# A decoder layer in float32: the first MLP matrix by seven products on half the tokens

## The reference

```python
h = rms_norm(x, norm_mix_pre[l])
m = hybrid_mixer(h, ...)                 # three parallel branches, gated, one output projection
x = x + rms_norm(m, norm_mix_post[l])
h = rms_norm(x, norm_ffn_pre[l])
f = jnp.square(jax.nn.relu(h @ w_ff1[l])) @ w_ff2[l]      # 1024 -> 4096 -> 1024
x = x + rms_norm(f, norm_ffn_post[l])
```

## Time and profile before

| | |
|---|---|
| Time, median of 3 runs | 987.01 us (986.59 to 987.07) |
| Profiled execution | 986.88 us; span from first to last instruction 985.1 us |
| TensorE busy | 965.7 us, 98% of the span, 4380 matmuls |
| VectorE, ScalarE, GpSimd busy | 674.5, 382.4, 98.6 us |
| MLP, first to last matmul | 645.36 to 977.43 us |
| DRAM read / written | 120.75 / 2.10 MB |

### The profile page before, as it was taken

One profiled execution on the slowest core, in us unless ns is written; L12 is line 12 of the kernel. 1 busy time (PEld: TensorE's weight loads), 2 busy tenths in 40 slices (PEclk: granted clock), 3 DMA queues, 4 the chain that ended last, 5 costly groups with the idle time before them and its releaser, 6 DMA issues.

```text
span 985.1 us, 12346 instructions
## 1 busy us (share of the span) xinstructions
PE 965.7 (98%) x4380; PEld 803.9 (82%) x4380; DVE 674.5 (68%) x829; ACT 382.4 (39%) x493; POOL 98.6 (10%) x115
## 2 busy tenths in 40 slices
PE   5999999999999999999999999999999999999996
PEld 4888888888888888888888888898888888888885
DVE  5348888889888988886584444656665674575568
ACT  5323333333333222224274223436534534543543
POOL 3000000000000001222200000220100100010012
PEclk9999999999999999999999999999999999999998
DMA  6323332232232222224226324155576487386453
GB/s 214 123 86 108 97 106 91 85 112 90 85 108 89 86 85 85 85 86 149 86 88 233 121 92 128 65 171 159 136 220 169 97 211 226 92 201 208 120 109 104
DMA packets 34629, 123.35 MB, mean 125 GB/s; under 512 B 4000, under 2 KB 4128, under 8 KB 34592
## 3 DMA queue, kind: packets, MB, share of 16 engines
q1 hardware_dynamic: 28368, 100.84, 29.8%
q0 software_dynamic: 5120, 17.83, 10.2%
q10 hardware_dynamic: 1104, 4.19, 1.2%
HBM read 120.75 MB, written 2.10 MB: 125 GB/s over the span
## 4 chain that ended last, share of the span: by engine, by line
PE 97%; DVE 1%; DMA 1%; issue 0%; ACT 0%; POOL 0%; POOLq 0%; DVEq 0%; ACTq 0%
PE ps L1147 31%; PE ps L1151 31%; PE ps L1149 31%; PE ps L1190 1%; PE ps L1304 1%; PE ps L1305 1%; PE ps L1303 1%; DMA conf<-x_in 1%; DVE wide L1080 0%; PE ps L1253 0%; PE ps L1254 0%; DVE wide L1093 0%; PE ps L1252 0%; DVE a_lo L765 0%; ACT ps L546 0%
## 5 line engine op out<-in xcount | busy, mean ns | idle before, releaser
L765 DVE TENSOR_TENSOR w_lo<-raw,w_hi 128x1024 fp32r<-128x1024 f32 x130 | 160.4, 1237 | 114.2 <-ACT w_hi L521 113.9
L1147 PE MATMUL ps<-a_hi,w_hi 128*128 128x512 f32 x576 | 225.4, 391 | 0.0
L1149 PE MATMUL ps<-a_lo,w_hi 128*128 128x512 f32 x576 | 224.2, 389 | 0.0
L1151 PE MATMUL ps<-a_hi,w_lo 128*128 128x512 f32 x576 | 224.1, 389 | 0.0
L521 ACT ACTIVATE w_hi<-raw 128x1024 fp32r<-128x1024 f32 x130 | 137.0, 1056 | 194.1 <-PE ps L1151 125.0
L842 DVE SCALAR_TENSOR_TENSOR conf<-glu,cols,conf (+1 forms) x240 | 186.9, 779 | 27.5 <-DVE conf L842 26.4
L1147 PE MATMUL ps<-b_hi,w_hi 128*128 128x512 f32 x360 | 140.2, 390 | 0.0
L1151 PE MATMUL ps<-b_hi,w_lo 128*128 128x512 f32 x360 | 140.1, 389 | 0.0
L1149 PE MATMUL ps<-b_lo,w_hi 128*128 128x512 f32 x360 | 140.1, 389 | 0.0
L1149 PEld LDWEIGHTS ps<-a_lo,w_hi 128*128 128x128 f32 x576 | 108.2, 188 | 22.6 <-issue 0.5
L1147 PEld LDWEIGHTS ps<-a_hi,w_hi 128*128 128x128 f32 x576 | 108.2, 188 | 22.6 <-DVE w_lo L765 0.2
(11 more groups left out here) (154 smaller groups left out, 1191.2 us busy)
## 6 DMA issues: line engine op xcount, KB each, us to landing
raw<-units_in SPq DMA_DIRECT2D x134, 512.0 KB, 3.3
glu<-units_in POOLq DMA_DIRECT2D x24, 512.0 KB, 5.5
raw_v<-units_in SPq DMA_DIRECT2D x22, 512.0 KB, 4.4
raw_c<-units_in SPq DMA_DIRECT2D x20, 512.0 KB, 4.0
glu<-units_in SPq DMA_DIRECT2D x8, 512.0 KB, 5.2
glu<-rows_in ACTq DMA_DIRECT2D x4, 512.0 KB, 10.7
conf<-x_in SPq DMA_DIRECT2D x4, 512.0 KB, 7.9
conf<-x_in ACTq DMA_DIRECT2D x1, 2048.0 KB, 9.1
```

What stands on the lines that cost most here:

```text
L765: return nc.vector.tensor_tensor(dst, src, hi, ALU.subtract)
L1147: nc.tensor.matmul(ps[:, bank, :], left_hi, right_hi, start=first, stop=False, skip_group_check=on_top)
L1149: nc.tensor.matmul(ps[:, bank, :], left_hi, right_lo, start=False, stop=False, skip_group_check=on_top)
L1151: return nc.tensor.matmul(ps[:, bank, :], left_lo, right_hi, start=False, stop=final, skip_group_check=on_top)
```

## The change

The up part uses seven products as well. The 1024 input channels and the 1024 hidden channels of a quarter are halved, and the tokens into 256 and 256. An up product has two units of 24 matmuls: 2 x 4 k-blocks x 3 on 256 tokens. There are 14 up units in a quarter instead of eight, and 28 in all instead of 22.

- The token side of the seven products (three plain blocks, four sums or differences, `xs_hi` and `xs_lo`) is made once, at the hand-off and in quarter 0's up part (`x_turned`, `x_difference_hi`, `x_lo`), and kept for all quarters.
- Hidden blocks `h11`, `h12`, `h21`, `h22` are sums of products: ScalarE copies a product out of PSUM (`keep`), VectorE adds another (`join`); relu, square, differences, and the seven sets of the down part follow (`rectify`, `difference`, `minus`, `set_hi`, `set_lo`).
- Products run in the order of `ORDER`; every down product goes by token tiles, and down product 2 stays in PSUM over all quarters (`is_read`).
- Raw slots are ten: up and down have slots of their own for the blocks that get additions. The two new ones lie in `conf`, so the mixed rows are stored to DRAM (`mixed_kept`) and loaded again for the end (`back`).
- Adding transfers: 16 in a quarter instead of 8; loads 16 instead of 18.

```diff
+ORDER = ((1, 2, 5, 3, 6, 7, 4), (5, 1, 2, 3, 6, 7, 4))
+SET_OF = {1: "11", 2: "12", 4: "22", 5: "22-21", 3: "21+12-11-22", 6: "21-22-11", 7: "11-21"}
+LOADED = {1: (0, 0), 2: (1, 0), 3: (1, 1), 5: (0, 0)}
+ADDED = {5: (0, 1), 6: (1, 1), 4: (1, 0), 7: (0, 1)}
+def slot_of(f, product):
+    return {1: 0, 2: 2, 3: 6, 7: 6}.get(product, 8 if f == DOWN else 4)
...
+            ff_load(0, UP, 1)
+            ff_load(0, UP, 2)
+            ff_load(0, UP, 5)
+            for c in range(CH):
+                sp.wait_ge(mixed_in, 4 * c + 4)
+                sp.dma_start(kept_d[c * P:(c + 1) * P, :], resid[:, c, :]).then_inc(mixed_kept[c], 16)
...
             for q in range(QUARTERS):
-                add_blocks(q, (5,))
-                add_blocks(q, (6,))
-                add_blocks(q, (7,))
-                add_blocks(q, (4,))
+                add_block(q, UP, 6)
+                if q == 0:
+                    add_block(0, DOWN, 5)
+                add_block(q, UP, 7)
+                add_block(q, UP, 4)
+                if q < QUARTERS - 1:
+                    add_block(q + 1, UP, 5)
+                for product in (6, 7, 4):
+                    add_block(q, DOWN, product)
+                if q < QUARTERS - 1:
+                    add_block(q + 1, DOWN, 5)
...
+            def keep(q, product, name, h=None):
...
+                nc.scalar.activation(dst, src, ACT.Copy).then_inc(kept, 1)
+            def rectify(q, n, name, sign):
+                h = h_of[name][:, :, :]
+                nc.scalar.activation(h, h, ACT.Relu, scale=sign).then_inc(rectified, 1)
+                act.wait_ge(rectified, 4 * q + n)
+                nc.scalar.activation(h, h, ACT.Square).then_inc(hidden, 1)
...
+                for h in range(2):
+                    done(q, UP, 7, h)
+                    split_behind(q, UP, 7, h)
+                act.wait_ge(hidden_diff, 4 * q + 1)
+                set_hi(q, "22-21")
+                act.wait_ge(joined, 5 * q + 5)
+                rectify(q, 3, "11", -1.0)
+                act.wait_ge(hidden, 4 * q + 3)
+                set_hi(q, "11")
...
+            def join(q, product, name, h=None):
...
+                nc.vector.tensor_tensor(at, src, at, ALU.add).then_inc(joined, 1)
...
+                    elif product == 7:
+                        dve.wait_ge(mlp_sum, sums_after(q, product, 1))
+                        for c in (0, 1):
+                            weigh(c, 1)
+                        dve.wait_ge(out_weighted, 4)
+                        for n in range(2):
+                            finish(n)
...
+            def up_unit(q, product, h, between=None):
+                u = ff_unit(q, UP, product, h)
+                hi, low = xs_hi[SET_OF[product]], xs_lo[SET_OF[product]]
+                ready(Count(u))
+                for e in range(2):
+                    out = ps[:, up_bank(q, product) + h, e * HALF_T:(e + 1) * HALF_T]
+                    free = on(product) or e == 1
+                    for k in range(CH):
+                        w = slice((CH * e + k) * P, (CH * e + k + 1) * P)
+                        nc.tensor.matmul(out, w_hi[:, u % RING, w], hi[:, k, :], start=not free and k == 0,
+                                         stop=False, skip_group_check=free)
...
+                    if e == 0 and between:
+                        between()
...
+                elif product in (3, 6):
+                    pe.wait_ge(kept, 5 * q + {3: 3, 6: 1}[product] + h)
+                elif product in (7, 4):
+                    pe.wait_ge(joined, 5 * q + {7: 2, 4: 4}[product] + h)
```

More of the change, by code:

```diff
@@ L114 @@
[L114 to L132, removed]
@@ L135, in ff_loads @@
[L135 to L141, removed]
-def source(u, added=False):
-    q, k = divmod(u - U_FF, PER_QUARTER)
-    product, h = piece_of(u)
-    if product is None:
-        return U_FF + 2 * KT * q + k
-    k_half, n_half = (ADDED if added else LOADED)[product]
-    return U_FF + 2 * KT * q + KT + CH * n_half + 2 * k_half + h
+HALF_T = SEQ // 2
@@ new lines, in earlier_in_slot, with ff_loads, sums_in_slot, source @@
+def earlier_in_slot(u):
+    return [v for v in range(U_FF, u) if ff_slot(v) == ff_slot(u)]
+def ff_loads(u):
+    before = U_FF // RAW if ff_slot(u) < RAW else 0
+    return 16 * (before + sum(piece_of(v)[2] in LOADED for v in earlier_in_slot(u)) + 1)
+def sums_in_slot(u):
+    return 16 * (sum(piece_of(v)[2] in ADDED for v in earlier_in_slot(u)) + 1)
+def source(u, added=False):
+    q, f, product, h = piece_of(u)
+    k_half, n_half = (ADDED if added else LOADED)[product]
+    if f == DOWN:
+        k_half = 1 - k_half
+    at = 2 * (2 * k_half + n_half) if f == UP else CH * n_half + 2 * k_half
+    return U_FF + (2 * q + f) * BLOCK_UNITS + at + h
@@ L280, in build, with set_over @@
[L280 removed]
+        raw_d = over("raw_d", [P, 2, D], "conf", 2 * D)
+        slots = [raw[:, 0, :], raw[:, 1, :], raw_v[:, 0, :], raw_v[:, 1, :], weighted, row[2],
+                 row[0], row[1], raw_d[:, 0, :], raw_d[:, 1, :]]
+        def set_over(name, first, skip=0, many=4):
+            return over(name, [P, many, CH, HALF_T], first, skip * D, dt=F32R)
+        x_plain_hi, x_plain_lo = set_over("x_plain_hi", "b_hi"), set_over("x_plain_lo", "b_lo")
@@ L1073, in half_of, with difference @@
+            def difference(q, n, first, second):
+                nc.vector.tensor_tensor(h_of[first if n == 1 else second][:, :, :], h_of[first][:, :, :],
+                                        h_of[second][:, :, :], ALU.subtract).then_inc(hidden_diff, 1)
             def half_of(n_half):
@@ new lines, in _ @@
+                split_behind(q, UP, 5, 1)
+                if q == 0:
+                    x_lo("21-22-11", 10)
+                set_lo(q, "22")
+                done(q, UP, 3, 0)
+                split_behind(q, UP, 3, 0)
+                if q == 0:
+                    x_lo("11-21", 11)
+                done(q, UP, 3, 1)
+                split_behind(q, UP, 3, 1)
+                dve.wait_ge(kept, 5 * q + 5)
+                for h in range(2):
+                    done(q, UP, 6, h)
+                    join(q, 6, "21", h)
+                    split_behind(q, UP, 6, h)
@@ new lines, in _ @@
+                done(q, UP, 7, 0)
+                dve.wait_ge(kept, 5 * q + 4)
+                join(q, 7, "11", 0)
+                dve.wait_ge(hidden, 4 * q + 2)
+                dve.wait_ge(set_lo_ready, len(H_ORDER) * q + 1)
+                difference(q, 1, "22", "21")
+                split_behind(q, UP, 7, 0)
+                done(q, UP, 7, 1)
+                join(q, 7, "11", 1)
+                split_behind(q, UP, 7, 1)
+                set_lo(q, "22-21")
+                set_lo(q, "11")
```

619 lines of the change are left out of this document (383 added, 236 removed).

## The result

The changed kernel takes 990.9 us (989.7 to 991.0, 7 runs), the kernel before 987.1 us on the same chip (986.6 to 987.2, 7 runs). The ratio is 1.0035, 95% interval 1.0025 to 1.0046: slower by 0.35%. The prediction said 984.6 us. The time lies inside its range, but the change went the other way.

What follows compares the result with a forecast made beforehand. The prediction took TensorE's matmul pace to bound the MLP. From the profiled 986.88 us it summed -17.5 + 3.8 + 10.5 + 0.9 to 984.6 us, range 975 to 996.

Steps and rivals of the forecast that it cites:

- Term 1: MLP matmuls: 256-column up matmuls at 0.1200 us each shorten the MLP from 332.1 to 314.6 us, -17.5 us.
- Term 2: Turn from up to down: VectorE's late splits stall TensorE before down product 2, 1.4 + 3 x 0.8 = +3.8 us.
- Term 3: Quarter 0's up part: queued adding transfers land late, the eighth at 688.2 us, delaying product 4; +10.5 us.
- Term 4: End of the program: VectorE reaches the last addition later, behind product 7's sums, weighting and two row finishings; +0.9 us.
- No effect for later quarters' transfers: Later quarters: additions go out in turn with the slots, the tightest found landing 4 us early; no cost, term 0.
- The turn rival: Turns from up to down: 2.3 us each instead of 0.8, or TensorE's half clock adds 4.5; 990 us, chance 0.14.
- Additions in time: Quarter 0's queue: it drains faster as stores and loads overlap, costing 3 instead of 10.5; 977 us, chance 0.17.
- DMA in every quarter: Every quarter: loads and additions don't overlap, so TensorE waits for DMA in each; 995 us, chance 0.12.
- both other paces: 256-column matmuls at the load pace, 0.112 (974 us, chance 0.02), or above the line, 0.131 (999 us, chance 0.05).
- The Trainium skill's gap: 256-column matmuls: N / 2.4 + 2.5 ns, 109 ns each, a first term of about -32 us; chance 0.02.

Runs made afterwards that it cites:

- plain transfers: Changed kernel with six of quarter 0's eight up-product additions, those behind the clearing, issued as plain transfers of the same pieces: 986.3 us, ratio 0.9988.
- the half-clock run: Changed kernel with 24 extra matmuls of 256 columns, result unread, ahead of up product 7's waits in quarter 0: 989.6 us, ratio 1.0027.
- the mix: Changed kernel without ScalarE's last-quarter waits for products 7 and 4, quarter 0's down product 5 additions one behind each of up product 4's: 980.5 us.
- the turn: Changed kernel with VectorE's fourth hidden difference moved behind the two splits that down product 2 waits for: 992.9 us, ratio 1.0053.

## Why the prediction was wrong

- **Term 1, the pace (-17.5): right.** 336 matmuls of 256 columns take 40.31 us in each of quarters 1 to 3, 0.1200 each. The line through 384 and 512 columns holds down to 256; whatever holds 128 columns at 0.1117 does not show there.
- **Term 2, the turn (+3.8): right, 3.3.** 0.75, 0.74, 0.70 and 1.07 by quarter, over the 38.08 that 168 matmuls of a down part take, released by VectorE's remainder, as the step said. Quarter 0 had no 1.4; there VectorE was no later than elsewhere. The working was too heavy in one place: VectorE is busy for 25.1 us in quarter 1's up part, where the step counted 29.8.
- **Term 3, quarter 0's additions (+10.5): the size right, 11.0 (9.8 to 10.5 in other traces with the same quarter 0), by two errors that cancel, which is luck.** The last split started at 685.57, so the eighth addition had landed some 2.6 us earlier than the 688.2 of the step; the queue drained faster than the step took it, and no run splits that between loads and additions. The clock then fell to half for 27 matmuls, which the step had taken as 0, since product 4 "waits for the landing anyway". It did not: there is no wait between products 7 and 4, and TensorE was the late one. The wait ahead of product 7 was 3.7 us, not 7; 3.1 stood ahead of product 3's two halves. The run with plain transfers takes 4.6 off; it makes the eight cheaper and does not remove them, so how much of the 11.0 the queue makes stays open. (A load is 1.48 by the step's own division, not 1.47, which changes nothing.)
- **Term 4, the end (+0.9): wrong, +7.4.** This step failed, and it alone turned the sign: 984.6 + 6.5 = 991.1, against 990.9 measured. The prediction put VectorE's own work at the end ("both sums of product 7, their weighting and the finishing of two rows") and priced it at its durations, 0.62 + 1.3 + 2.8 "+ waits", without following those waits. The finishing waits for GpSimd, GpSimd for ScalarE's squares, and ScalarE's stream has two waits ahead of them that the kernel before had not. And what the step did price cost nothing: with ScalarE's two waits gone and VectorE's order as it is, the end is 7.8 us, against 7.7 before the change. Its sign, a last addition over 1 us behind the last matmul, came true, at 7.9, for a reason that the step had not named. Followed through, the sum was to be had from rows of before and the code: squares behind the last matmul, six of them at 0.61, then `rstd`, two finishings, and two additions, each behind the other.
- **No effect for later quarters' transfers: right.** With a DMA share of 0.95 in quarter 1's up part (0.60 over the MLP before) TensorE waits there for nothing.
- **The rivals.** None described this. The turn rival's 990 lies next to the 990.9, but by luck: its turns cost 3.3 us in all and not 2.3 each, and the half clock that it offers besides cost 2.5 of its 4.5 and lies inside the 11.0. "Additions in time", "turn", "DMA in every quarter" and both other paces are excluded by the same rows.

The Trainium skill's gap (TensorE: Matmul & The Clock Gate, Back-to-back issue gap) was given 2 in 100 and did not hold: 120.0 ns at 256 columns, where its formula, which the section calls that of an isolated matmul, gives 109.

## What to carry to other kernels

Price the end of a program by going backwards through every engine's stream, and list each wait that stands ahead of the last useful work: a loop that is written for a steady state ("wait until the product is done, then split") costs nothing there and 7.4 us in its last turn, where the work behind the wait has gone. Where the DMA engines are full, putting a queue in the order in which its items are wanted was worth 3.5 us, and two further orders nothing. And where TensorE stands still, look at the granted clock behind it: here idle times of 1.75 to 4.6 us had a stretch at half clock behind them, which cost 1.5 to 2.5 us in quarter 0's up part on top of the wait.

## What the runs showed of the hardware

- A matmul of 256 columns with its own weight load of 128 goes every 120.0 ns in this format, on the line of 384 and 512 columns (one column per cycle at 2.4 GHz and 13.3 ns more).
- The granted clock fell to 0.50 behind an idle time of 3.7 us and was so from 683.4 to 689.3 us, with TensorE busy without a gap. In four more traces with idle times of 3.7 to 4.6 us in the same place the half clock lasted 3.4 us, 16 matmuls. It fell too behind 1.75 us (the mix), 1.8 us (the turn) and 1.9 us (plain transfers: 0.57 over the 3 us that follow), and not behind 1.7 us (changed kernel, ahead of product 3's second half) and 1.4 us (the half-clock run, ahead of product 7).
- A DMA share of 0.95 over the 40 us of quarter 1's up part cost TensorE nothing, since each transfer was ahead of its use. An adding transfer of 512 KB took 5.5 us to land at the median before the change and 6.7 to 8.5 (by slot) in the changed kernel, with a DMA share of 0.84 over the MLP instead of 0.60.
